# GpSimd and ScalarE stop normalizing k: its norm goes into the gates' exponent, in a gated DeltaNet layer

## The chip, the cores and the metric

The kernel runs on one core of one Trainium2 chip. The metric is the device time of one execution in microseconds (us). Engines are named PE (TensorE, matmuls), DVE (VectorE), ACT (ScalarE), POOL (GpSimd) and SP (SyncE, which issues the DMAs).

## The reference, cut to what matters

One inference step of a two-layer decoder for 512 prompt tokens and 8 single decode tokens (520 columns in all). Layer 0 is a pooling and differential attention mixer, layer 1 a gated DeltaNet mixer with 8 heads; each is followed by a SwiGLU feed-forward. The change lies in layer 1:

```
q = l2_normalize(conv[..q]) * (GDN_DK ** -0.5)
k = l2_normalize(conv[..k])                      # x * rsqrt(sum(x*x) + EPS)
g = -exp(a_log) * softplus(a + dt_bias);  beta = sigmoid(b)
Gc = cumsum(g)                                   # within a chunk
decay = exp(where(i >= j, Gc_i - Gc_j, -inf));  gam = exp(Gc)
M = I + where(i > j, beta_i * (k_i . k_j) * decay, 0)
W = M^-1 (beta * gam * k);   U = M^-1 (beta * v)
qk = (q_i . k_j) * decay;    k_dec = exp(Gc_last - Gc) * k
per chunk:  u = U - W S;  o = (gam q) S + qk u;  S = g_last * S + k_dec^T u
```

## The kernel before, in words

**Layout.** Features lie on the 128 partitions, tokens in the columns. Weights come as f32 units of 1 MB through two `stage` slots, are split into two f16 parts by ACT (`wh`) and DVE (`wl`), and each product is three f16 matmuls by k tile (`wh·zh`, `wh·zl`, `wl·zh`), each in two halves of 260 columns. All engines run hand-written programs in a fixed order; semaphores alone join them, so an instruction that waits holds up everything behind it on its own engine.

**The head loop.** Layer 1's mixer is a loop over the 8 heads, `for h in range(HG)`, on every engine. PE does in head h the DeltaNet work of head h and, between its dependent steps, the projection of head h + 1, cut in 32 parts of 6 matmuls (`fill(n)` does the next n parts; `project_part`, line L2110). In order, PE's head is: `gb_ps`, where a selector matrix spreads the head's rows of cumulated log gates (bank 2) and of beta (bank 3) to all partitions (L2230, f32 at L2222 in head 0), with the same for the 8 decode tokens (L2233); `stat_head` (L2094), the sums for the output norm of head h - 1; `kk_ps` and `qk_ps` (both L2119), k times k and k times q by 128-token chunks; two transposes `n_ps` and `tk_ps` (both L2125); six doubling steps of the triangular inverse, `level(l)`, each a product `z_ps` (L2288), a transpose `x_ps` (L2296) and a product `v_ps` (L2303); at last four chunk steps with `ws_ps` (L2331), `u_ps` (L2315), `ds_ps` (L2345) and the output products (L2347, L2351). In level 0 the decode tokens' products stand as well (L2264 to L2268).

**The norm of k.** After the convolution and SiLU of head p = h + 1, POOL squares k (`square_k`), PE sums the squares over the partitions with a matrix of ones (`stat_l2(p)`, L2087, in the third chunk step of head h), ACT takes Ln and Exp of it (`norm_l2`, L996 and L998) and POOL multiplies k by the result (`normalize_k`, L643). DVE then makes beta·k in `kbg_w` (L1581), which is the left side of `kk_ps`. DVE's exponent of the decay is `et` (four instructions, L1575); ACT takes its Exp (L1053), DVE makes `nt_z`, the off-diagonal matrix (L1586), from which `level` starts. ACT evacuates its transpose to `nf_u` (L1045), POOL makes six copies of pieces of that (`offs`, L709), one for each level, and then multiplies `kbg_w` by `gamB`, the exponent of the gates (L712), gates the output of head h - 1 (L661) and q (L716).

**Other work named below.** `leave` (L1438) scales a finished projection tile; `convolve` (L1453, L1456) is a tap of the convolution; `head_scale` (L1522) belongs to the output norm; `split_quarter` (L1486) is a quarter of DVE's weight split; `next_split` (L761) is ACT's whole weight split of a unit. L1602 evacuates `z_ps`, L1628 takes `v_ps` off the inverse, L1672 is the step of the state S, L1120 ACT's evacuation of the head's output.

## Time and profile before

| | |
|---|---|
| median of 3 runs | 1335.24 us (1335.07 to 1337.36) |
| the profiled execution's own time | 1334.86 us |
| its span in the trace | 1332.9 us |
| granted PE clock, mean | 0.998 |
| busy: PE, PE's weight loads, DVE, ACT, POOL | 98%, 81%, 48%, 38%, 27% |
| DMA traffic over the span | 140.89 MB, mean 106 GB/s |

Busy shares are over the span; the kernel's own time is about 2 us longer, for what lies around it. A matmul's end is modelled with its pipeline, so the records of neighbouring matmuls overlap; what a matmul costs PE is the distance from its start to the next one's start.

### The profile page before, as it was taken

Reading aid. Unit: us, or ns where it says so; the run is one execution under the profiler, and the core shown is the slowest. Engines: PE = TensorE matmul, PEld = TensorE weight load, DVE = VectorE, ACT = ScalarE, POOL = GpSimd, SP = SyncE. Lnnn points to the kernel's source line nnn. Section 1 sums busy time; section 2 is a strip of 40 time slices with the busy share of each in tenths; the row PEclk is TensorE's granted clock in tenths of the full one; section 3 lists DMA queues with packets and bytes.
Section 4 is the critical chain, followed back from the end, with each engine's and each line's share of the span. In section 5 each row is a group of like instructions: output and inputs, shape, how many; then the busy total and the mean of one; then the engine's idle time right before and its main releaser. Section 6 shows DMA issues by size and latency. Waiting matters only on the chain.

```text
span 1332.9 us, 28024 instructions
## 1 busy us (share of the span) xinstructions
PE 1309.3 (98%) x11596; PEld 1086.3 (81%) x11596; DVE 634.4 (48%) x1009; ACT 507.1 (38%) x785; POOL 365.9 (27%) x506
## 2 busy tenths in 40 slices
PE   8999999999999999999999999999999999999997
PEld 7766588888888888887778777877888888888886
DVE  5447653333333322267776677766633333332222
ACT  6243453222222322244555465545432223222221
POOL 1004324121212100165453545453221222211010
PEclk9999999999999999999999999999999999999999
DMA  8658422422232232111212221122223222233211
GB/s 264 209 191 278 143 96 95 149 102 99 94 122 104 101 121 85 63 64 40 89 41 88 88 72 57 73 96 66 96 105 116 94 94 94 94 118 131 88 44 64
DMA packets 32140, 140.89 MB, mean 106 GB/s; under 512 B 4634, under 2 KB 6938, under 8 KB 20155
## 3 DMA queue, kind: packets, MB, share of 16 engines
q1 hardware_dynamic: 32058, 139.75, 30.2%
q8 instruction: 58, 0.95, 0.3%
q14 instruction: 24, 0.19, 0.0%
HBM read 128.63 MB, written 11.11 MB: 105 GB/s over the span
## 4 chain that ended last, share of the span: by engine, by line
PE 92%; DVE 4%; ACT 1%; issue 1%; DMA 1%; SPq 0%; DVEq 0%; ACTq 0%
PE P L1745 64%; PE P L2110 10%; PE P L2303 2%; DVE wl L1486 1%; PE P L2288 1%; PE P L2365 1%; PE P L2296 1%; PE P L2119 1%; PE P L1823 1%; PE P L2125 1%; PE P L2331 1%; PE P L2345 1%; PE P L1955 1%; PE P L2321 1%; PE P L1898 1%
## 5 line engine op out<-in xcount | busy, mean ns | idle before, releaser
L1745 PE MATMUL P<-zh,wh 128*128 128x260 f16 x1712 | 329.2, 273 | 2.1 <-DVE wl L1194 2.1
L1745 PE MATMUL P<-zl,wh 128*128 128x260 f16 x1712 | 329.0, 273 | 0.0
L1745 PE MATMUL P<-zh,wl 128*128 128x260 f16 x1712 | 329.0, 273 | 0.0
L1174 DVE SCALAR_TENSOR_TENSOR wl<-stage,wh 128x2048 f16<-128x2048 f32 (+1 forms) x75 | 185.3, 2471 | 195.4 <-ACT wh L761 192.8
L1745 PE MATMUL P<-arena,wh 128*128 128x260 f16 x1816 | 276.2, 273 | 1.0 <-DVE hT L1391 0.3
L1745 PEld LDWEIGHTS P<-arena,wh 128*128 128x128 f16 x1816 | 175.0, 97 | 29.2 <-issue 1.3
L1745 PEld LDWEIGHTS P<-zh,wh 128*128 128x128 f16 x1712 | 164.3, 97 | 34.0 <-issue 6.7
L1745 PEld LDWEIGHTS P<-zh,wl 128*128 128x128 f16 x1712 | 165.6, 97 | 25.9
L1745 PEld LDWEIGHTS P<-zl,wh 128*128 128x128 f16 x1712 | 165.4, 97 | 25.8
L1745 PE MATMUL P<-arena,wl 128*128 128x260 f16 x908 | 174.5, 273 | 0.0
L761 ACT ACTIVATE wh<-stage 128x2048 f16<-128x2048 f32 (+1 forms) x80 | 161.8, 2023 | 3.6 <-PE P L1745 3.6
L564 POOL TENSOR_TENSOR arena<-arena 128x520 f32<-128x520 f32 x44 | 56.5, 1284 | 359.7 <-DVE arena L1411 359.7
L1411 DVE TENSOR_TENSOR arena<-P,rstd 128x520 f32<-128x520 f32 x88 | 61.2, 696 | 171.8 <-PE P L1745 168.8
L965 ACT ACTIVATE arena<-arena 128x520 f32 (+1 forms) x44 | 28.0, 637 | 198.9 <-POOL arena L564 198.9
L1745 PEld LDWEIGHTS P<-arena,wl 128*128 128x128 f16 x908 | 87.9, 97 | 13.6
L523 POOL TENSOR_TENSOR ssq<-ssq,sq 128x520 f32<-128x520 f32 x27 | 36.8, 1364 | 212.1 <-ACT sq L770 211.9
L2110 PE MATMUL P<-zh,wh 128*128 128x260 f16 x448 | 86.9, 275 | 0.0
L2110 PE MATMUL P<-zl,wh 128*128 128x260 f16 x448 | 86.1, 273 | 0.0
L2110 PE MATMUL P<-zh,wl 128*128 128x260 f16 x448 | 86.1, 273 | 0.0
L961 ACT ACTIVATE arena<-arena 128x520 f32<-128x520 f32 x44 | 28.0, 637 | 129.6 <-DVE arena L1411 129.6
L777 ACT ACTIVATE zh<-hT,par 128x520 f16<-128x520 f32 x24 | 17.4, 726 | 120.9 <-DVE hT L1391 109.2
L1486 DVE SCALAR_TENSOR_TENSOR wl<-stage,wh 128x512 f16<-128x512 f32 x64 | 59.8, 944 | 0.0
(366 smaller groups left out, 1646.3 us busy)
## 6 DMA issues: line engine op xcount, KB each, us to landing
stage<-w_gu SPq DMA_DIRECT2D x44, 1024.0 KB, 4.8
stage<-w_in SPq DMA_DIRECT2D x23, 1024.0 KB, 4.9
stage<-w_dn SPq DMA_DIRECT2D x16, 1408.0 KB, 5.8
arena<-cache_k SPq DMA_DIRECT2D x32, 256.0 KB, 3.5
stage<-w_out SPq DMA_DIRECT2D x8, 1024.0 KB, 5.4
arena<-cache_v SPq DMA_DIRECT2D x32, 256.0 KB, 3.0
arena<-delta_state SPq DMA_DIRECT2D x8, 512.0 KB, 3.5
o_ds<-arena SPq DMA_DIRECT2D x8, 512.0 KB, 6.8
```

The costliest lines, as they stand in the source:

```text
L523: ins = nc.gpsimd.tensor_tensor(ssq[:, :], ssq[:, :], sq[:, k % 2, :], ADD)
L564: nc.gpsimd.tensor_tensor(gu[:, j, :], gt[:, j, :], ut[:, j, :], MUL).then_inc(prod_done, 1)
L761: nc.scalar.activation(wh[:, j, 0:words], stage[:, j, 0:words], ACT.Copy, scale=WS).then_inc(hi_ready, 1)
L777: nc.scalar.activation(zh[:, k, :], hT[:, k, :], ACT.Copy, scale=par[:, NORM[b] + k:NORM[b] + k + 1]).then_inc(z_hi, 1)
L961: nc.scalar.activation(gt[:, j, :], gt[:, j, :], ACT.Silu).then_inc(silu_done, 1)
L965: nc.scalar.activation(fh[:, bass.ds(2 * i + j, 1), :], gu[:, j:j + 1, :], ACT.Copy).then_inc(f_hi, 1)
L1174: nc.vector.scalar_tensor_tensor(out=wl[:, j, 0:words], in0=stage[:, j, 0:words], scalar=WS, in1=wh[:, j, 0:words], op0=MUL, op1=SUB).then ...
L1411: nc.vector.tensor_tensor(paired(dst[:, j, :]), pm[j], paired(rstd[:, :]), MUL).then_inc(pm_free, 1)
L1486: ins = nc.vector.scalar_tensor_tensor(out=wl[:, j, q], in0=stage[:, j, q], scalar=WS, in1=wh[:, j, q], op0=MUL, op1=SUB)
L1745: mm = nc.tensor.matmul(pm[j][:, c, :], w[:, wslot, o:o + 128], x[:, k, c * CH:(c + 1) * CH], start=(k == first and w is wh and x is xh), ...
L2110: mm = nc.tensor.matmul(pm[0][:, c, :], w[:, u % 2, o:o + 128], x[:, k, c * CH:(c + 1) * CH], start=(k == 0 and w is wh and x is zh), stop ...
L2303: mm = nc.tensor.matmul(v_out[:, c % 2, 64 * m:64 * m + 64], dt2_x[r, 128 * m:128 * m + 128], nt_z[r, 64 * m:64 * m + 64], start=True, sto ...
```

## The change

k is left as it is after the SiLU. With n_i = |k_i|², log n_i and log beta_i go into the exponent of the decay, and what is solved for is scaled by |k_i| (`kn`, in place of beta, on v). The diagonal of k·k is the sum of squares, so the norm is read from `kk_ps` (four reductions with an identity matrix on DVE). Beta's row is no longer spread over the prompt's columns; its logarithm comes with the transposed rows (`tokm`). Decode tokens get their norms from one product with the matrix of ones (`qkk`), now 16 columns and part of `gb_ps`. The sum of squares on POOL, `stat_l2`, `norm_l2`, `normalize_k` and DVE's beta·k go. GpSimd now makes `kbg_w` from k and `gamB` (`gate_k`), behind its six copies, as it did the gating of `kbg_w` before. Several orders move: `kk_ps` ahead of `gb_ps`, `add_query` from the end of a head into the next one, ACT's weight split ahead of the Exp of `et`, ACT's load of the SiLU tables behind `Kd`, and the number of projection parts at six places.

```
@@ GpSimd @@
-            def square_k(h):
...
-            def normalize_k(h):
-                pool.wait_ge(nrs, h + 1)
-                x = qkvc[:, h % 2, 1, :]
-                nc.gpsimd.tensor_tensor(x, x, rs2[:, 1, :], MUL).then_inc(nq, 1)
+            def decode_products(h):
+                pool.wait_ge(csilu, 3 * h + 2)
+                if h >= 1:
+                    pool.wait_ge(kqs_ps, h)
+                    pool.wait_ge(*G("gb_ps", h))
+                q, k = qkvc[:, h % 2, 0, SEQ:], qkvc[:, h % 2, 1, SEQ:]
+                nc.gpsimd.tensor_copy(kd2, two(k))
...
+                nc.gpsimd.tensor_tensor(qkk[:, 0:8], q, k, MUL)
+                nc.gpsimd.tensor_tensor(qkk[:, 8:16], k, k, MUL).then_inc(dprep, 1)
+            def gate_k(h):
+                pool.wait_ge(*G("gam", h + 1))
+                if h >= 1:
+                    pool.wait_ge(*G("ws_ps", 3 * h))
+                nc.gpsimd.tensor_tensor(kbg_w, qkvc[:, h % 2, 1, 0:SEQ], gamB, MUL).then_inc(k_gated, 1)
@@ GpSimd, loop @@
                 for l in range(LEVELS):
                     nc.gpsimd.tensor_copy(packed(l, offs[l]), early(l, nf_u)).then_inc(S["om"], 1)
-                pool.wait_ge(*G("gam", h + 1))
-                pool.wait_ge(*G("kk_ps", h + 1))
-                nc.gpsimd.tensor_tensor(kbg_w, kbg_w, gamB, MUL).then_inc(S["kbg"], 1)
+                gate_k(h)
@@ ACT, loop @@
                 act.wait_ge(*G("gb_ps", h + 1))
-                nc.scalar.activation(gamB, P[:, 2, :], ACT.Exp).then_inc(S["gam"], 1)
                 nc.scalar.activation(gD[:, h, :], P[:, 7, 0:8], ACT.Exp).then_inc(S["gd"], 1)
+                nc.scalar.activation(rk, P[:, 7, 24:32], ACT.Ln, bias=epsc[:, 2:3]).then_inc(S["lr"], 1)
+                act.wait_ge(*G("dg", h + 1))
+                nc.scalar.activation(klog, ksq, ACT.Ln, bias=epsc[:, 2:3]).then_inc(S["lk"], 1)
+                act.wait_ge(*G("lr", h + 1))
+                nc.scalar.activation(rk, rk, ACT.Exp, scale=-0.5)
+                nc.scalar.activation(qks, P[:, 7, 16:24], ACT.Copy).then_inc(S["rk"], 1)
+                if h >= 1:
+                    next_split("in1", h, 1)
                 act.wait_ge(*G("ex", h + 1))
                 nc.scalar.activation(et, et, ACT.Exp).then_inc(S["et"], 1)
                 nc.scalar.activation(kd4, d4, ACT.Exp).then_inc(S["kd4"], 1)
+                act.wait_ge(*G("lk", h + 1))
+                nc.scalar.activation(kn, klog, ACT.Exp, scale=0.5).then_inc(S["kn"], 1)
...
-                next_split("in1", h, 1)
+                nc.scalar.activation(gamB, P[:, 2, :], ACT.Exp).then_inc(S["gam"], 1)
@@ DVE, loop @@
-                dve.wait_ge(*G("gd", h + 1))
+                dve.wait_ge(*G("kk_ps", h + 1))
+                for c in range(4):
+                    ins = nc.vector.tensor_tensor_reduce(out=dg_out[c], in0=P[:, 6, c * 128:(c + 1) * 128], in1=ident[:, :],
+                                                         scale=1.0, scalar=0.0, op0=MUL, op1=ADD,
+                                                         accum_out=ksq[:, c:c + 1])
+                ins.then_inc(S["dg"], 1)
+                dve.wait_ge(*G("lk", h + 1))
+                link(nc.vector.tensor_tensor(tj, tokg[:, :, h], klog, ADD))
...
-                nc.vector.tensor_copy(bD[:, h, :], P[:, 7, 8:16]).then_inc(S["bd"], 1)
-                dve.wait_ge(nq, h + 1)
-                nc.vector.tensor_tensor(kbg_w, P[:, 3, :], k, MUL).then_inc(S["kb"], 1)
+                dve.wait_ge(*G("rk", h + 1))
+                nc.vector.tensor_tensor(br, P[:, 7, 8:16], rk, MUL).then_inc(S["bd"], 1)
+                if n >= 0:
+                    add_query(n)
                 convolve(h, 2, 0)
-                convolve(h, 2, 1)
@@ PE, loop @@
+                pe.wait_ge(csilu, 3 * h + 2)
+                if h >= 1:
+                    pe.wait_ge(*G("u", 4 * h))
+                chunks(6, k, k, "kk_ps")
...
-                    for m, t in enumerate((g3, b3)):
-                        nc.tensor.matmul(P[:, 2 + m, :], sel3[0:72, h % 2, :], t[0:72, 0:SEQ], start=True, stop=True)
+                    nc.tensor.matmul(P[:, 2, :], sel3[0:72, h % 2, :], g3[0:72, 0:SEQ], start=True, stop=True)
...
+                pe.wait_ge(dprep, h + 1)
+                nc.tensor.matmul(P[:, 7, 16:32], ones[:, :], qkk, start=True, stop=True).then_inc(S["gb_ps"], 1)
                 fill(4 if h < HG - 1 else 3)
+                ready(h, "gd", "rk", "bd")
+                chunks(7, k, q, "qk_ps")
+                ready(h, "kn")
                 if h >= 1:
-                    pe.wait_ge(nln, h + 1)
+                    pe.wait_ge(snew, h)
                     stat_head(h - 1)
-                pe.wait_ge(nq, h + 1)
-                ready(h, "kb")
...
-                        if c == 2:
+                        if c == 2 and h == HG - 1:
                             pe.wait_ge(snew, h + 1)
-                            if h + 1 < HG:
-                                stat_l2(h + 1)
...
                     if c == 0:
-                        fill(3)
+                        fill(2 if h < HG - 1 else 3)
```

PE's order at the turn from one head to the next (heads 1 and 2), before. The row before the first is the last output product; `head_act`, `head_dve` and the like are the semaphores on which the other engines count their head tiles:

```order
L2351 MATMUL P<-arena 128x128
L2230 MATMUL P<-arena 128x512 [waits head_dve,head_pool]
L2230 MATMUL P<-arena 128x512
L2233 MATMUL P<-arena 128x8 [waits head_act]
L2233 MATMUL P<-arena 128x8
...
L2094 MATMUL P<-ssq,onesH 128x260 [waits o1sum,nln]
L2094 MATMUL P<-ssq,onesH 128x260
L2119 MATMUL P<-arena 128x128 [waits head_dve,nq]
L2119 MATMUL P<-arena 128x128 x3
L2119 MATMUL P<-arena 128x128 [waits head_dve,head_act]
L2119 MATMUL P<-arena 128x128 x3
```

And of the changed kernel at the same place (L2124 is `chunks`, L2236 the gates' selector, L2242 the product with ones, L2099 `stat_head`):

```order
L2350 MATMUL P<-arena 128x128
L2124 MATMUL P<-arena 128x128 [waits head_act,csilu]
L2124 MATMUL P<-arena 128x128 x3
L2236 MATMUL P<-arena 128x512 [waits head_dve,head_pool]
L2239 MATMUL P<-arena 128x8 [waits head_act]
L2239 MATMUL P<-arena 128x8
L2242 MATMUL P<-arena,ones 128x16 [waits dprep]
...
L2124 MATMUL P<-arena 128x128 [waits head_dve,head_act]
L2124 MATMUL P<-arena 128x128 x3
L2099 MATMUL P<-ssq,onesH 128x260 [waits o1sum,snew,head_act]
L2099 MATMUL P<-ssq,onesH 128x260
```

The k·k products moved to the head's first place, one selector matmul of 512 columns went, and the sums of `stat_head` now also wait for ACT (`kn`).

ACT's order in the front of head 2, before (L1050 is `gamB`, L1051 `gD`, L1053 `et`, L1055 the copy of the identity, L761 the weight split, L1027 and L1029 `head_factor`):

```order
L1050 ACTIVATE arena<-P 128x512 [waits head_pe]
L1051 ACTIVATE arena<-P 128x8
L1053 ACTIVATE arena<-arena 128x512 [waits head_dve]
L1054 ACTIVATE arena<-arena 128x4
L1055 ACTIVATE arena<-ident 128x512
L761 ACTIVATE wh<-stage 128x2048 [waits mm_done,w_in1]
L1027 ACTIVATE arena<-P,epsc 128x520 [waits o1stat]
```

And of the changed kernel (L1046 to L1051 are the logarithms and factors of the norms, L763 the weight split, L1055 `et`, L1058 `kn`, L1062 `gamB`):

```order
L1045 ACTIVATE arena<-P 128x8 [waits head_pe]
L1046 ACTIVATE arena<-P,epsc 128x8
L1048 ACTIVATE P<-arena,epsc 128x4 [waits head_dve]
L1050 ACTIVATE arena<-arena 128x8 [waits head_act]
L1051 ACTIVATE arena<-P 128x8
L763 ACTIVATE wh<-stage 128x2048 [waits mm_done,w_in1]
L1055 ACTIVATE arena<-arena 128x512 [waits head_dve]
L1056 ACTIVATE arena<-arena 128x4
L1058 ACTIVATE arena<-P 128x4 [waits head_act]
L1059 ACTIVATE arena<-ident 128x512
L1062 ACTIVATE arena<-P 128x512
L1021 ACTIVATE arena<-P,epsc 128x520 [waits o1stat]
```

The weight split moved from behind the Exp of `et` to ahead of it, and `gamB` from first to nearly last.

## Rows read from the trace of the kernel before

**Rows 1.** The page: busy time by engine, and the chain that ended last.

```profile
PE 1309.3 (98%) x11596; PEld 1086.3 (81%) x11596; DVE 634.4 (48%) x1009; ACT 507.1 (38%) x785; POOL 365.9 (27%) x506
...
PE 92%; DVE 4%; ACT 1%; issue 1%; DMA 1%; SPq 0%; DVEq 0%; ACTq 0%
```

**Rows 2.** Windows, one head: length, PE, PEld, DVE, ACT, POOL; clock, DMA share, GB/s.

```profile
681.00:725.00 44.00, 43.26 (x405) 34.73 (x404) 31.88 (x69) 23.55 (x50) 20.48 (x37) 1.00 0.21 73
```

**Rows 3.** Timeline of PE, front of head 2 (start, duration, line, shapes, records).

```profile
678.96 0.39 PE L2351 MATMUL P<-arena 128*128 128x128 f32 x2
679.43 0.59 PE L2230 MATMUL P<-arena 72*128 72x512 bf16 x2
680.04 0.20 PE L2233 MATMUL P<-arena 72*128 72x8 bf16 x2
680.14 0.38 PE L2110 MATMUL P<-zh,wh 128*128 128x260 f16 x2
...
682.82 1.04 PE L2094 MATMUL P<-ssq,onesH 128*128 128x260 f32 x4
683.69 1.95 PE L2119 MATMUL P<-arena 128*128 128x128 f32 x16
...
689.13 0.46 PE L2288 MATMUL P<-arena 128*64 128x64 f32 x8
```

**Rows 4.** Timeline of PE, third chunk step of head 2: `stat_l2` and what follows.

```profile
717.92 1.04 PE L2087 MATMUL P<-sq,ones 128*128 128x260 f32 x4
718.79 0.38 PE L2315 MATMUL P<-arena 128*128 128x128 f32 x2
```

**Rows 5.** Timeline of PE, where head 0 begins.

```profile
589.46 1.04 PE L2087 MATMUL P<-sq,ones 128*128 128x260 f32 x4
...
590.71 1.96 PE L2222 MATMUL P<-arena 40*128 40x512 f32 x4
592.51 0.51 PE L2224 MATMUL P<-arena 40*128 40x8 f32 x4
```

**Rows 6.** Timeline of DVE, front of head 2 and its levels 0 and 1.

```profile
678.94 0.35 DVE L1672 SCALAR_TENSOR_TENSOR arena<-arena,P 128x128 f32<-128x128 f32 x1 [1.50 <-PE P L2345]
...
681.30 1.12 DVE L1575 SCALAR_TENSOR_TENSOR arena<-P,arena 128x128 f32<-128x128 f32 x4
...
689.63 0.29 DVE L1602 TENSOR_TENSOR arena<-P,arena 128x128 f32<-128x128 f32 x1
...
692.44 0.49 DVE L1628 TENSOR_TENSOR arena<-arena,P 128x128 f32<-128x128 f32 x2 [0.92 <-PE P L2303]
692.84 1.60 DVE L1486 SCALAR_TENSOR_TENSOR wl<-stage,wh 128x512 f16<-128x512 f32 x1
```

**Rows 7.** Timeline of ACT, front of head 2.

```profile
679.38 0.60 ACT L1120 ACTIVATE arena<-P 128x512 f32<-128x512 f32 x1 [1.06 <-PE P L2351]
...
681.03 0.17 ACT L1051 ACTIVATE arena<-P 128x8 f32<-128x8 f32 x1
...
683.67 1.89 ACT L761 ACTIVATE wh<-stage 128x2048 f16<-128x2048 f32 x1
```

**Rows 8.** Timeline of DVE in layer 0: the kernel's other multiply-and-reduce.

```profile
43.81 0.29 DVE L1243 CUSTOM_DVE_ANT_0 arena<-P,arena 128x128 f32<-128x128 f32 x1 [1.60 <-PE P L1823]
44.03 0.08 DVE L1243 DVE_READ_ACCUMULATOR2_ANT arena<- 128x1 f32 x1
```

**Rows 9.** Timeline of POOL in head 2: the six copies, the gating of `kbg_w`.

```profile
688.12 2.86 POOL L709 COPY arena<-arena 128x256 f32<-128x256 f32 x6 [4.94 <-ACT arena L1045]
690.94 1.70 POOL L712 TENSOR_TENSOR arena<-arena 128x512 f32<-128x512 f32 x1
```

**Rows 10.** Timeline of DVE ahead of head 0: the gates' rows.

```profile
581.27 0.69 DVE L1471 TENSOR_TENSOR arena<-arena 8x520 f32<-8x520 f32 x1
...
586.60 0.13 DVE L1478 COPY arena<-arena 8x8 f32<-8x8 f32 x1
```

**Rows 11.** Timeline of ACT ahead of head 0: the SiLU of q and k.

```profile
586.77 1.16 ACT L1005 ACTIVATE arena<-arena 128x520 f32<-128x520 f32 x2
```

More of the change, by code:

```diff
@@ L63 @@
 HEAD_TILES = {
-    "pe": ["gb_ps", "kk_ps", "qk_ps", "n_ps", "tk_ps"] + ["z_ps", "x_ps", "v_ps"] * 4 + ["z_ps", "tv_ps", "x_ps", "v_ps"] +
+    "pe": ["kk_ps", "gb_ps", "qk_ps", "n_ps", "tk_ps"] + ["z_ps", "x_ps", "v_ps"] * 4 + ["z_ps", "tv_ps", "x_ps", "v_ps"] +
           ["z_ps", "x_ps", "v_ps"] + ["u_ps", "ds_ps"] + ["ws_ps", "u_ps", "ds_ps"] * 3 + ["o_ps"],
-    "act": ["gam", "gd", "et", "kd4", "yi", "ye", "nf", "kd", "x"] + ["ye", "x"] * 4 + ["bv", "ye", "x"] + ["u"] * 4 + ["o"],
-    "dve": ["ex", "bd", "kb", "nt", "xt", "at"] + ["z", "xt"] * LEVELS + ["s"] + ["r", "s"] * 3,
-    "pool": ["selb"] + ["om"] * LEVELS + ["kbg", "qd"],
+    "act": ["gd", "lr", "lk", "rk", "et", "kd4", "kn", "yi", "gam",
+            "ye", "nf", "kd", "x"] + ["ye", "x"] * 4 + ["bv", "ye", "x"] + ["u"] * 4 + ["o"],
+    "dve": ["dg", "ex", "bd", "nt", "xt", "at"] + ["z", "xt"] * LEVELS + ["s"] + ["r", "s"] * 3,
+    "pool": ["selb"] + ["om"] * LEVELS + ["qd"],
 }
@@ L201, in hybrid_trunk @@
         qq = [sq[:, 0, :], rs2[:, 0, :]]
-        gD, bD = (a2(64).rearrange("p (h b) -> p h b", h=HG) for _ in range(2))
+        tokg = rs2[:, 1, 0:32].rearrange("p (c n) -> p c n", c=4)
+        ksq, kn, tj = (rs2[:, 1, 32 + 4 * i:36 + 4 * i] for i in range(3))
+        klog = P[:, 4, 400:404]
+        rk, br, qks = (rs2[:, 1, 48 + 8 * i:56 + 8 * i] for i in range(3))
+        gD = a2(64).rearrange("p (h b) -> p h b", h=HG)
         gate = a2(8)
@@ L222, in hybrid_trunk @@
         tailw = ddt.bitcast(f16).rearrange("p (m k n c) -> p m k n c", m=2, k=KD - EARLY_K, n=2)
+        dg_out = [t[:, i:i + 128] for t in (dt2_x, ya) for i in (256, 384)]
         bf40 = [t.bitcast(mybir.dt.bfloat16) for t in (yn1[:, 0:260], yn1[:, 260:520], ors1[:, 0:260])]
@@ L706, in _ @@
                                         ).then_inc(sdec, 1)
+                if h == 0:
+                    tail_of(0, 2)
+                    decode_conv(0, (2,))
                 pool.wait_ge(*G("nf", h + 1))
@@ L1063, in _ @@
                 evac(nf_u, 3, "n_ps", "nf", h)
-                act.preload_act_table(ACT.Silu)
                 act.wait_ge(*G("tk_ps", h + 1))
@@ L1070, in _ @@
                 ins.then_inc(S["kd"], 1)
+                act.preload_act_table(ACT.Silu)
                 for l in range(LEVELS):
@@ L1113, in _ @@
                         act.preload_act_table_set("natural_log_exp_and_others")
-                    if c == 2 and p < HG:
-                        norm_l2(p)
                 if p < HG:
@@ L2083, in _ @@
             unit("in1", 0, 1, zh, zl)
-            def stat_l2(h):
-                pe.wait_ge(nsq, h + 1)
-                for c in range(2):
-                    mm = nc.tensor.matmul(stat[:, c, :], ones[:, :], sq[:, 1, c * CH:(c + 1) * CH],
-                                          start=True, stop=True)
-                mm.then_inc(nstat, 1)
             def stat_head(h):
@@ L2143, in stat_last @@
                 mm.then_inc(o1stat, 1)
-            stat_l2(0)
             pe.wait_ge(rows_ready, 2)
             for c in range(4):
-                mm = nc.tensor.transpose(P[:, 6, 40 * c:40 * c + 40], rows[0:40, c * 128:(c + 1) * 128],
+                mm = nc.tensor.transpose(P[:, 5, 40 * c:40 * c + 40], rows[0:40, c * 128:(c + 1) * 128],
                                          ident[0:40, 0:40])
@@ L2220, in _ @@
                 if h == 0:
-                    for m in range(2):
-                        nc.tensor.matmul(P[:, 2 + m, :], selb[0:40, m, :], rows[0:40, 0:SEQ], start=True, stop=True)
+                    nc.tensor.matmul(P[:, 2, :], selb[0:40, 0, :], rows[0:40, 0:SEQ], start=True, stop=True)
                     for m in range(2):
@@ L2266, in between @@
                                              start=True, stop=True)
-                        nc.tensor.matmul(P[:, 4, 256:264], ones[:, :], qkp, start=True, stop=True)
                         nc.tensor.transpose(P[0:36, 4, 264:392], kpad[:, 0:36], ident[:, :]).then_inc(kqs_ps, 1)
```

104 lines of the change are left out of this document (42 added, 62 removed).

## The prediction

> **What bounds the kernel now.** I read the page first: PE is busy for 98% of the span and makes up 92% of the chain that ended last, while no other engine passes 48% [rows 1]. So what the change takes off DVE, ACT or POOL is worth nothing by itself; it counts where it takes matmuls off PE, or where PE stands still. Next the windows, one per head: in 44.0 us PE is busy 43.26, so at most 0.74 us a head is plainly idle, at full clock [rows 2]. Then the timelines of the engines around the turn from head 1 to head 2, for the waits inside those 0.74 us.
>
> There the reader should take starts, not durations, since ends are modelled. Eight 128-column f32 matmuls take 0.22 us each at PE (683.69, and the parts behind them); `stat_l2` with its two of 260 columns takes 717.92 to 718.79, 0.87 us [rows 3, 4]. The last output product starts at 678.96, so PE could go on at 679.18. It goes on at 679.43, just after DVE's state step L1672 ends at 679.29: 0.25 us idle. The two selector matmuls (512 columns each, 0.22 us by the same pace of columns) are through by 679.87, and the small ones start at 680.04, behind ACT's evacuation, which ends at 679.98: 0.17 us idle [rows 3, 6, 7]. Four projection parts then take 680.14 to 682.82, 0.67 us each, and level 0 starts at 689.13 [rows 3].
>
> **What the change removes from PE.** `stat_l2` goes eight times (once ahead of head 0, then in heads 0 to 6): 8 x 0.87 = 7.0 us [rows 4, 5]. It stood between two chunk steps, where a projection part of 0.67 us now fills the wait, moved there from the first chunk step; the parts are 32 in either kernel, so they cost nothing more. Beta's selector matmul goes eight times: in head 0 it is f32, half of 590.71 to 592.51, 0.90 us; in the others 0.22 us [rows 5]. The product with ones gets 16 columns for 8 and moves from level 0 to the front; I leave its cost unchanged, some 0.2 us like a short matmul pair, at either place.
>
> **What it does to the front of a head**, in head 2's times, as if it began at the same 679.18. Now `kk_ps` comes first: 0.89 us, to 680.07. It covers both waits, the one on L1672 and the one on ACT's evacuation. Selector 0.22, small ones 0.1, ones 0.2: 680.6, against 680.14 before. Four parts: 683.27. Meanwhile the new chain runs:
> - DVE, four reductions. The trace has the same kind of instruction over a 128x128 block: 0.22 us from one to the next, then 0.08 for the accumulator [rows 8]. 4 x 0.22 + 0.08 = 0.95, so 680.17 to 681.1.
> - ACT, the logarithm of four numbers: 0.17, like the 8-column L1051 [rows 7]; 681.3. DVE, the sum `tj`, 0.2 with its link; then the four `et` instructions, 1.12 [rows 6]; `ex` and `bd` end with two short ones at 0.15, a little over L1478's 0.13 [rows 10]: 682.9. PE asks for `bd` at 683.27, so it is hidden, with 0.35 us to spare.
> - ACT, in the same time: three short ones (681.1 to 681.6), the weight split 1.89 [rows 7] to 683.5, Exp of `et` 0.60 (512 columns, like L1120), `kd4` and `kn` at 0.17: 684.45. PE is through with `qk_ps` at 684.16 and asks for `kn` ahead of `stat_head`: a new wait of 0.3 us. Behind that wait stand `stat_head`, one part and the transpose `n_ps`; POOL's copies wait for the latter's evacuation.
> - PE goes on: `stat_head` 0.87, one part 0.67, two transposes of four blocks each (0.11 us a block, a single pass) 0.88, three parts 2.0: level 0 at 688.9, against 689.13. 0.23 us are gained, and 0.2 more in level 0, where the ones product no longer stands.
>
> DVE has then to keep up in levels 0 and 1. It has one tap more between `At` and the tile that it must free, but it waited 0.92 us for PE in level 0 [rows 6], and it loses beta·k. `decode_update` gets one short instruction more (0.2 us), inside a wait of DVE for PE. POOL: `gate_k` is one instruction of the size of the one it replaces, at the same place, 1.70 us behind 2.86 us of copies [rows 9], and nobody asks for it before the second chunk step, far later. POOL's squares and its normalization end, and were waited for by nobody late. All of this costs nothing, by the cover named.
>
> **Sum.** Heads 1 to 6: 0.43 + 0.87 = 1.30 us each, 7.8. Head 7 has no `stat_l2`: 0.43. Head 0: 0.87 ahead of it, 0.90 for the selector, 0.87 in it, 2.64; against that two new waits. The rows of beta need three more DVE instructions (0.48, 0.48 and 0.69, the size of L1471) ahead of ACT's Exp, and another of 0.69 behind, so what ended at 586.60 ends some 2.5 us later, about when PE is through at 589.46; the SiLU of q and k, at 586.77, moves by some 2 us, and `kk_ps` waits for it to 589.95: 0.5 us [rows 5, 10, 11]. In head 0 the split of weights still stands ahead of the logarithms, so `bd` is about 0.35 us late. Head 0: 1.8 us. Together 10.0 us. The profiled execution took 1334.86 us, which gives 1324.8; the median of the runs is 0.4 above it, so I say 1325.
>
> **Bounds.** The chain's unknown is how fast three engines hand short work to each other. Below: nothing is late, `kn` included (0.3 us less a head, 2 us in all), and head 0's waits vanish: 1322. Above: every step of the new chain takes twice as long (the reductions 1.9 for 0.95), given below as a rival. I take the rows' values, since the reduction is seen in this very kernel.
>
> **Rivals.**
> - *The new chain is late* (18%). With reductions of 1.9 us `bd` comes at 683.9 (0.6 us of wait), the split ends at 684.45 and `kn` comes at 685.4, 0.65 us after PE's `qk_ps`: 1.25 us idle for 0.3, so 0.95 us a head over seven heads, 6.7 us back: 1331.5. For it: the chain crosses PE, DVE, ACT, DVE, ACT, PE within 5 us. Against: the parts cover 2.7 of these.
> - *The front's gain is lost in levels 0 and 1* (14%). There DVE's weight split takes 1.60 us, and PE waits for DVE rather than the other way round. If POOL, whose copies start when ACT has evacuated `n_ps`, and DVE stay where they are, 0.43 us a head go, 3.4 us: 1328.5. The Trainium skill, "SBUF — State Buffer", on who interferes with whom, says that a DVE instruction with two SBUF inputs and a GpSimd instruction that reads SBUF exclude each other for the whole of an instruction. As a mechanism of this kernel: the third tap moves under the six copies, 0.48 us each (2.86 / 6), and DVE could come one or two copies late to the evacuation of `z_ps` [rows 9]. By that rule it is 0.5 to 1 us late. PE needs that evacuation only after a transpose and a part, so about 1.2 us are free, and by this the sum stays as it is.
> - *Slower* (7%). In the trace the weight split starts at 683.67, behind the Exp of `et` [rows 7]; nothing shows that its weights were there earlier. In the changed kernel `et` stands behind it. Were the split possible only then, it would end at 685.56, `kn` would come at 686.5, and PE would stand 2.35 us for 0.3: 7 x 2.05 = 14.4 us, more than the whole gain: 1339. It decides from 683.67 - 681.6 - (10.0 / 7) on, that is, if the weights are there later than 683.0. Against: that half of `stage` was freed in the head before, and DMA is nearly idle here, 0.21 of its time [rows 2].
> - *No difference* (5%): the first two together, and head 0 worse than reckoned: 1333 to 1336.
> - Forecast as summed (56%): 1322 to 1327.
>
> **Range and chances.** The forecast's range is 1322 to 1327. With the two rivals above it, 8 in 10 lie from 1321.5 to 1331.5. Within 0.2% (2.7 us), about what a measurement of this kernel can tell from no change, of the time before, lie the no-difference case and the edge of the first rival: 0.07. Slower: 0.07. Faster: the rest of the first rival, the second and the forecast, 0.86.
>
> **What would show it.** In the profile after: a head from start to start of `et`'s group takes about 42.6 us, not 43.9; PE's first f32 group after the output products has no idle ahead of it; eight groups of `stat_l2` are gone and nothing stands in their place; the gap ahead of `stat_head` is about 0.3 us and is put down to ACT; the gap ahead of `qk_ps` is nothing in heads 1 to 7 and some 0.35 us in head 0. The prediction fails if PE stands for over 1 us in the front of each head, or if the waits of levels 0 and 1 on DVE grow by what the front gained.

## The result, and the profile after

The changed kernel takes 1320.14 us (median of 4 runs, 1318.96 to 1322.66) against 1335.15 us (median of 4) for the kernel before in the same measurement: a ratio of 0.9885, 95% interval 0.9872 to 0.9899. It is faster by 15.0 us where 10.2 were forecast, and lies below the forecast's range and below the one of 8 in 10. The profiled execution took 1319.1 us, its span is 1317.4 us, 15.5 less than before; the forecast's sum was 10.0.

The page of the changed kernel, with the lines that answer to [rows 1]:

```profile
PE 1297.6 (98%) x11555; PEld 1078.9 (82%) x11555; DVE 641.4 (49%) x1086; ACT 501.3 (38%) x809; POOL 351.7 (27%) x498
...
PE 94%; DVE 3%; issue 1%; DMA 1%; ACT 1%; SPq 0%; DVEq 0%
```

PE's busy time fell by 11.7 us and the span by 15.5: more waiting went than the forecast's list contains.

Next, a head is cut in three pieces, all read from starts in PE's timeline: **front**, from the end of the last output product (its start and 0.22 us) to the first `z_ps` (level 0); **levels 0 and 1**, up to the `z_ps` of level 2; and the rest. PE, changed kernel, where [rows 3] stood (last output product, `kk_ps`, selector, small ones, ones product, first part, `qk_ps`, `stat_head`, and the `z_ps` of levels 0, 1 and 2):

```profile
673.76 0.39 PE L2350 MATMUL P<-arena 128*128 128x128 f32 x2
673.98 1.06 PE L2124 MATMUL P<-arena 128*128 128x128 f32 x8
674.87 0.38 PE L2236 MATMUL P<-arena 72*128 72x512 bf16 x1
675.09 0.19 PE L2239 MATMUL P<-arena 72*128 72x8 bf16 x2
675.14 0.37 PE L2242 MATMUL P<-arena,ones 128*128 128x16 f32 x2
675.37 0.38 PE L2115 MATMUL P<-zh,wh 128*128 128x260 f16 x2
...
678.05 1.05 PE L2124 MATMUL P<-arena 128*128 128x128 f32 x8
679.03 1.14 PE L2099 MATMUL P<-ssq,onesH 128*128 128x260 f32 x4
...
683.66 0.46 PE L2289 MATMUL P<-arena 128*64 128x64 f32 x8
...
687.09 0.45 PE L2289 MATMUL P<-arena 128*64 128x64 f32 x8
...
689.97 0.45 PE L2289 MATMUL P<-arena 128*64 128x64 f32 x8
```

The front is 673.98 to 683.66, 9.68 us, and PE goes from the output product into `kk_ps` with no gap. And PE of the kernel before in levels 0 and 1 of the same head (rows that were not shown ahead of the prediction): the `z_ps` of level 1, then two instructions that wait for DVE. Ahead of them, in level 0, the transpose `x_ps`.

```profile
690.65 0.41 PE L2296 MATMUL P<-ident,arena 128*128 128x128 f32 x2
...
693.03 0.45 PE L2288 MATMUL P<-arena 128*64 128x64 f32 x8
...
694.79 0.66 PE L2303 MATMUL P<-arena 64*128 64x64 f32 x8 [0.25 <-DVE arena L1602]
...
696.57 0.45 PE L2288 MATMUL P<-arena 128*64 128x64 f32 x8 [0.34 <-DVE arena L1628]
```

`x_ps` starts 0.32 us behind the last of the decode tokens' products (690.33). It waits for ACT's `Kd` (L1068, to 690.51), which stands behind the load of the SiLU tables:

```profile
688.07 1.28 ACT L1064 ACT_TABLE_LOAD   x1
689.37 1.14 ACT L1068 ACTIVATE arena<-P,arena 128x128 f32<-128x128 f32 x4
```

In the changed kernel `Kd` ends at 683.41, before z0, and the same distance is 0.12 us (684.62 to 684.74).

By head, in us (z0, z1, z2: start of the `z_ps` of levels 0, 1, 2). A head is counted from its z0 to the next head's, so the front in its row is the one that leads to the next head:

| | front | z0 to z1 | z1 to z2 | rest | head |
|---|---|---|---|---|---|
| before, every head from 1 to 5 | 9.95 | 3.90 | 3.53 | 26.50 | 43.88 |
| changed, heads 1, 2, 3, 5 ("quick") | 9.68 | 3.43 | 2.87 | 25.62 | 41.60 |
| changed, head 4 ("long") | 9.68 | 4.05 | 3.38 | 25.62 | 42.73 |
| forecast | 9.72 | 3.70 | 3.53 | 25.63 | 42.58 |

Front and rest came as forecast. Levels 0 and 1, where only the 0.2 us of the moved ones product had been expected, gave 1.13 us in a quick head and nothing in a long one. Head 6 is long too (4.06 and 3.37). Outside the table, the front of head 1 took 10.28 us before and takes 9.68 now. The windows from z0 to z2, a quick head (2) and a long one (4) of the changed kernel; columns as in [rows 2]:

```profile
683.66:689.97 6.31, 6.31 (x79) 4.63 (x78) 5.83 (x12) 3.73 (x9) 6.31 (x8) 1.00 0.01 4
766.87:774.30 7.43, 6.50 (x79) 4.66 (x78) 7.33 (x12) 3.73 (x9) 6.43 (x8) 1.00 0.01 2
```

The clock is full in both, DMA is silent, the same instructions run. What differs is DVE: 7.33 us busy for 5.83 with the same 12 instructions, and PE stands for 0.93 us.

DVE in these two stretches, first the quick head, behind the dots the long one (L1528 `head_scale`, L1492 a quarter of the weight split, L1642 the subtraction off the inverse):

```profile
684.58 0.75 DVE L1528 SCALAR_TENSOR_TENSOR arena<-arena,par 128x520 f32<-128x520 f32 x1
685.25 0.88 DVE L1492 SCALAR_TENSOR_TENSOR wl<-stage,wh 128x512 f16<-128x512 f32 x1
686.50 0.49 DVE L1642 TENSOR_TENSOR arena<-arena,P 128x128 f32<-128x128 f32 x2 [0.37 <-PE P L2304]
686.91 0.92 DVE L1492 SCALAR_TENSOR_TENSOR wl<-stage,wh 128x512 f16<-128x512 f32 x1
...
767.79 1.01 DVE L1528 SCALAR_TENSOR_TENSOR arena<-arena,par 128x520 f32<-128x520 f32 x1
768.72 1.75 DVE L1492 SCALAR_TENSOR_TENSOR wl<-stage,wh 128x512 f16<-128x512 f32 x1
770.40 0.47 DVE L1642 TENSOR_TENSOR arena<-arena,P 128x128 f32<-128x128 f32 x2
770.79 1.38 DVE L1492 SCALAR_TENSOR_TENSOR wl<-stage,wh 128x512 f16<-128x512 f32 x1
```

And POOL (L714 the six copies, L683 `gate_k`, L667 the gating of the output), first the quick head, then the long one:

```profile
682.45 3.15 POOL L714 COPY arena<-arena 128x256 f32<-128x256 f32 x6 [4.74 <-ACT arena L1038]
685.56 1.71 POOL L683 TENSOR_TENSOR arena<-arena 128x512 f32<-128x512 f32 x1
687.22 1.74 POOL L667 TENSOR_TENSOR arena<-arena 128x520 f32<-128x520 f32 x1
...
765.66 2.59 POOL L714 COPY arena<-arena 128x256 f32<-128x256 f32 x6 [4.74 <-ACT arena L1038]
768.21 1.71 POOL L683 TENSOR_TENSOR arena<-arena 128x512 f32<-128x512 f32 x1
```

PE in the long head, the `z_ps` of levels 1 and 2:

```profile
770.92 0.45 PE L2289 MATMUL P<-arena 128*64 128x64 f32 x8 [0.55 <-DVE arena L1642]
...
774.30 0.45 PE L2289 MATMUL P<-arena 128*64 128x64 f32 x8 [0.34 <-DVE arena L1642]
```

Read them side by side. The first split quarter takes 0.88 us in the quick head and 1.75 in the long one. In the quick head the six copies take 3.15 us, so the sixth ends 1.9 us after z0 and DVE's quarter, begun 1.6 us after z0, has gone ahead of `gate_k`. In the long head the copies take 2.59, `gate_k` begins 1.34 us after z0, the quarter is begun 0.51 us behind it, and ends 0.55 us after `gate_k` is over. So I read them thus: the two engines take turns instruction by instruction; who begins first has it, and the other's record grows by what it waited.

### The profile page after: what moved, and what is told of

The parts are those of the page before. It is cut to its first block, busy times and chain, and to the rows that moved or that the text cites. A ratio compares the mean times of both kernels' runs of the same rounds, so it can differ in the third digit from the quotient of the medians.

```text
span 1317.4 us, 27997 instructions
## 1 busy us (share of the span) xinstructions
PE 1297.6 (98%) x11555; PEld 1078.9 (82%) x11555; DVE 641.4 (49%) x1086; ACT 501.3 (38%) x809; POOL 351.7 (27%) x498
## 4 chain that ended last, share of the span: by engine, by line
PE 94%; DVE 3%; issue 1%; DMA 1%; ACT 1%; SPq 0%; DVEq 0%
PE P L1757 65%; PE P L2115 11%; PE P L2304 2%; PE P L2289 1%; PE P L2124 1%; PE P L2364 1%; PE P L2130 1%; PE P L2297 1%; DMA hT<-xT 1%; PE P L2333 1%; PE P L1835 1%; PE P L2344 1%; PE P L2322 1%; PE P L1967 1%; DVE wl L1492 1%
## 5 line engine op out<-in xcount | busy, mean ns | idle before, releaser
L763 ACT ACTIVATE wh<-stage 128x2048 f16<-128x2048 f32 (+1 forms) x80 | 161.8, 2023 | 3.6 <-PE P L1757 3.6
L1492 DVE SCALAR_TENSOR_TENSOR wl<-stage,wh 128x512 f16<-128x512 f32 x64 | 60.1, 949 | 0.0
```

Of the source, the lines that this page charges most:

```text
L763: nc.scalar.activation(wh[:, j, 0:words], stage[:, j, 0:words], ACT.Copy, scale=WS).then_inc(hi_ready, 1)
L1492: ins = nc.vector.scalar_tensor_tensor(out=wl[:, j, q], in0=stage[:, j, q], scalar=WS, in1=wh[:, j, q], op0=MUL, op1=SUB)
```

## The experiments

Theory A, formed from these rows: in levels 0 and 1 PE doesn't set the pace. Three long instructions of POOL and four quarters of DVE shut each other out, and what PE has there is partly slack. Most of the 1.13 us of a quick head came since DVE now comes in time. Theory B: PE sets the pace there too, and the surplus comes from PE's own work. Ratios are to the kernel before on the same chip. "Head" is the length of the heads between 1 and 5 unless said otherwise.

**A product as long as `stat_l2`, back in the third chunk step** (four f32 matmuls of 128 columns with a matrix of ones, result unused, in heads 0 to 6):

```
+                        if c == 2 and h < HG - 1:
+                            for i in range(4):
+                                nc.tensor.matmul(P[:, 4, 0:128], ones[:, :], onesH[:, :], start=True, stop=True)
```

> The changed kernel with four f32 matmuls of 128 columns more (a matrix of ones, 0.88 us by the trace's 0.22 each) in the third chunk step of heads 0 to 6, where stat_l2 stood. Both theories expect the same here: nothing else moves, each head is 0.88 us longer, 6.2 us in all, 1326.3 against the changed kernel's 1320.1. It prices the removed sums.

Measured: 1325.53 us, ratio 0.9922 [0.9906, 0.9937]. Heads are 42.50 (quick) and 43.62 (long): 0.9 more of each kind. There PE's work costs its full length, as the sum had it.

**The same four matmuls in level 0** of the changed kernel:

```
                     if l == 0:
                         pe.wait_ge(sdec, h + 1)
+                        if h < HG - 1:
+                            for i in range(4):
+                                nc.tensor.matmul(P[:, 6, 0:128], ones[:, :], onesH[:, :], start=True, stop=True)
```

> The same four matmuls, but in level 0 of heads 0 to 6. Theory (the extra gain is a matter of phase between DVE's weight split and GpSimd's gating: when PE and DVE come to level 1 earlier, the split at L1492 starts ahead of GpSimd's gating of the output and takes 0.9 us instead of 1.6): DVE's second split quarter starts after GpSimd's second long instruction and takes 1.6 us again, so the matmuls cost more than their own 0.88, about 1.4 to 1.5 us a head, 10 to 10.8 us in all, 1330 to 1331. Rival (PE alone sets the head): 0.88 us a head as in the third chunk step, 1326.3.

Measured: 1324.69 us, 0.9922 [0.9905, 0.9939]. Levels 0 and 1 are 4.52 + 2.91 = 7.43 us in every steady head: 1.13 more than a quick head, and nothing more than a long one. At this place the four matmuls take 1.09 us from start to start (685.57 to 686.66 in head 2), so a quick head pays for them in full, and no more. What I expected of DVE did not happen: its second quarter takes 0.97 us, not 1.6, and it is the first that takes 1.76, as in a long head. The total is 5 to 6 us under what I expected, and under the rival's too: a head paid 1.13 us and not 1.4 to 1.5, and I had not counted that the changed kernel has long heads already.

**And in level 0 of the kernel before**, the same edit:

> The kernel before with the four f32 matmuls of ones (0.88 us on PE) added in level 0 of heads 0 to 6. Theory (in the kernel before, level 0 to level 2 takes 7.43 us because GpSimd's three long instructions and DVE's three weight split quarters take turns, and PE has slack there): the matmuls cost at most 0.1 to 0.2 us a head, level 0 to 2 stays within 7.4 to 7.6 us, 1335.2 to 1336.5 in all. Rival (PE sets the time there too, as it is busy for 98%): 0.88 us a head, 6.2 us, 1341.4.

Measured: 1336.6 us, 1.0006 [0.9997, 1.0015]; heads of 44.00 us. The four matmuls, 1.09 us from start to start here too (692.65 to 693.74), cost 0.12 us a head. Theory B asked for 0.88 a head, 6 us in all, and falls: 0.97 us of the 1.09 went into waiting that was already there. Levels 0 and 1 are 4.75 + 2.81 us. DVE in head 2 of this kernel, and behind it POOL:

```profile
696.43 0.49 DVE L1628 TENSOR_TENSOR arena<-arena,P 128x128 f32<-128x128 f32 x2 [1.77 <-PE P L2306]
696.83 0.75 DVE L1486 SCALAR_TENSOR_TENSOR wl<-stage,wh 128x512 f16<-128x512 f32 x1
```

```profile
695.74 1.29 POOL L661 TENSOR_TENSOR arena<-arena 128x520 f32<-128x520 f32 x1
696.99 1.72 POOL L716 TENSOR_TENSOR arena<-arena 128x512 f32<-128x512 f32 x1
```

DVE now waits 1.77 us for PE, where it waited 0.92 [rows 6], and its quarter takes 0.75 us where it took 1.60: it asks at 696.83, just ahead of POOL's handover at 696.99, and hardly waits.

**`gate_k` ahead of the six copies, changed kernel:**

```
+                gate_k(h)
                 pool.wait_ge(*G("nf", h + 1))
                 for l in range(LEVELS):
                     nc.gpsimd.tensor_copy(packed(l, offs[l]), early(l, nf_u)).then_inc(S["om"], 1)
-                gate_k(h)
```

> The changed kernel with gate_k ahead of the six copies instead of behind. Theory (phase): GpSimd's two remaining long instructions then run 1.7 us earlier, the gating of q holds from about 12.9 to 14.6 us after the head's start, just as DVE's second split quarter (12.93) wants to begin; that one ends at about 15.2 instead of 13.85 and PE comes 0.5 to 0.7 us later to level 2: 3.5 to 5 us slower in all, 1324 to 1325. Rival (any instruction of GpSimd taken off that stretch only helps DVE, or does nothing): 1317 to 1320.

Measured: 1322.18 us, 0.9893 [0.9877, 0.9909]. All steady heads are alike, 41.95 us (3.43 + 3.22). So the order on POOL alone changes the length of level 1, by 0.35 us against a quick head where I had said 0.5 to 0.7, and the total is 2 us under what I expected.

**The same in the kernel before** (the gating of `kbg_w` ahead of the copies):

```
+                pool.wait_ge(*G("gam", h + 1))
+                pool.wait_ge(*G("kk_ps", h + 1))
+                nc.gpsimd.tensor_tensor(kbg_w, kbg_w, gamB, MUL).then_inc(S["kbg"], 1)
                 pool.wait_ge(*G("nf", h + 1))
                 for l in range(LEVELS):
                     nc.gpsimd.tensor_copy(packed(l, offs[l]), early(l, nf_u)).then_inc(S["om"], 1)
-                pool.wait_ge(*G("gam", h + 1))
-                pool.wait_ge(*G("kk_ps", h + 1))
-                nc.gpsimd.tensor_tensor(kbg_w, kbg_w, gamB, MUL).then_inc(S["kbg"], 1)
```

> The kernel before with its gating of kbg_w ahead of the six copies. Theory (phase): in it the third split quarter takes 1.55 us behind GpSimd's gating of q; with that gating 1.7 us earlier it takes 0.7, while the second stays near 1.6. PE comes 0.5 to 0.8 us earlier to level 2 in heads 1 to 7: 1330 to 1332 against 1335.2. Rival (the head is set by PE, GpSimd's place has no part in it): 1335.

Measured: 1332.64 us, 0.9975 [0.9966, 0.9984], heads of 43.16 us (3.90 + 2.81). One instruction moved on an engine that is busy for 27% of the span takes 0.72 us off a head, all of it in level 1. Level 0 keeps its 3.90. The median lies a little above the 1330 to 1332 that I expected.

**POOL's long instructions out of levels 0 and 1**, changed kernel, `gate_k` and the gating of q held until level 2:

```
-                gate_k(h)
                 if n >= 0:
                     gate_out(n)
+                pool.wait_ge(*G("z", LEVELS * h + 3))
+                gate_k(h)
```

> The changed kernel, but on GpSimd the output's gating comes right behind the six copies, and gate_k and the gating of q wait until DVE has passed the evacuation of level 2's first product (a wait on DVE's counter), so that they don't meet DVE's three weight split quarters of levels 0 and 1. Theory (whichever of GpSimd's long two-input instructions and DVE's split comes first holds up the other; a head of the changed kernel takes 41.61 us when the copies end late and 42.73 us when gate_k starts ahead of the first quarter): the quarters take 0.7 to 0.9 us, level 0 to level 2 takes at most the 6.3 us of the quick heads in every head, no head takes 42.7; 1317 to 1319 and less spread. Rival (the long heads come from something else, such as the order of ACT): two kinds of heads stay, 1320 to 1321.

Measured: 1345.82 us, 1.0078 [1.0065, 1.0091], slower than the kernel before. Levels 0 and 1 did as theory A says, 3.43 + 2.81 = 6.24 us in heads 0 to 6 and quarters of 0.68 to 0.99 us. But level 2 went from 3.01 to 5.16 us. DVE there, in head 2 (the update for the decode tokens):

```profile
693.86 0.17 DVE L1541 TENSOR_TENSOR arena<-P,arena 128x8 f32<-128x8 f32 x1
694.06 1.10 DVE L1542 TENSOR_TENSOR arena<-arena 128x8 f32<-128x8 f32 x1
695.19 1.19 DVE L1543 TENSOR_TENSOR arena<-arena 128x8 f32<-128x8 f32 x1
696.42 1.09 DVE L1544 TENSOR_TENSOR arena<-arena 128x8 f32<-128x8 f32 x1
```

and POOL beside it (L683 `gate_k`, L720 the gating of q, L671 the low f16 part of the gated output):

```profile
693.87 1.27 POOL L683 TENSOR_TENSOR arena<-arena 128x512 f32<-128x512 f32 x1 [3.44 <-DVE arena L1617]
695.09 1.27 POOL L720 TENSOR_TENSOR arena<-arena 128x512 f32<-128x512 f32 x1
696.32 1.17 POOL L671 TENSOR_TENSOR arena<-arena 128x520 f16<-128x520 f32 x1
```

Three instructions of 8 columns, 0.17 us each in the changed kernel, take 1.09 to 1.19 us: each ends just after the POOL instruction beside it. In two of the heads the cost was larger still, which the last section tells.

**`gate_k` ahead, only the gating of q held until level 2:**

```
+                gate_k(h)
                 pool.wait_ge(*G("nf", h + 1))
...
-                gate_k(h)
...
+                pool.wait_ge(*G("z", LEVELS * h + 3))
                 pool.wait_ge(*G("qk_ps", h + 1))
```

> The changed kernel with gate_k ahead of the six copies and only the gating of q held until DVE has passed level 2's evacuation. Theory: as above, one long instruction (the output's gating, 1.28 us) is left near the quarters; level 0 to level 2 at most 6.3 us, 1317 to 1319. Rival (gate_k ahead costs what it cost in gate_ahead_after, whatever follows): 1322.

Measured: 1330.5 us, 0.9952 [0.9938, 0.9965]. Levels 0 and 1 again 6.24, level 2 at 4.14 to 4.31: the same collision, one POOL instruction smaller (in head 2 two of DVE's 8-column instructions take 1.10 and 1.09 us). Both expectations were wrong in the total for the same reason: I had moved POOL's work without asking what DVE does where it lands.

**The load of the SiLU tables back ahead of `Kd`, changed kernel:**

```
                 evac(nf_u, 3, "n_ps", "nf", h)
+                act.preload_act_table(ACT.Silu)
...
                 ins.then_inc(S["kd"], 1)
-                act.preload_act_table(ACT.Silu)
```

> The changed kernel with ACT's load of the SiLU tables put back ahead of Kd. Theory (the 0.2 us between the decode products and the transpose x_ps of level 0 was PE's wait for Kd, and went because the load of 1.28 us moved): the gap is back at 0.2 us a head, or more since PE now comes earlier, 1.6 us or some more in all by itself: 1321.5 to 1323. Rival (the gap was something else): 1320.

Measured: 1321.99 us, 0.9889 [0.9875, 0.9904]; two steady heads of 41.82 (3.71 + 2.81), the other three long. Level 0 is 0.28 us longer and level 1 gives 0.06 back, so in a head that is not long the edit costs 0.22 us. PE's distance ahead of `x_ps` is 0.37 us there (645.47 to 645.84, head 1) for 0.12. The total fits what I expected, but says little, since more heads are long here than in the first profile of the changed kernel.

**The table load behind `Kd`, and the SiLU of z behind `x`'s evacuation, kernel before:**

```
-                act.preload_act_table(ACT.Silu)
...
                 ins.then_inc(S["kd"], 1)
+                act.preload_act_table(ACT.Silu)
...
-                    else:
-                        silu_z(h)
...
                     if l == 0:
+                        silu_z(h)
                         silu_v(h)
```

> The kernel before with only the one order changed: ACT's load of the SiLU tables behind Kd, and the SiLU of z behind the evacuation of x_ps. Theory (PE's 0.2 us ahead of x_ps in level 0 is a wait for Kd): it goes, 0.2 us a head from level 0 to level 1, 1.6 us in all, 1333.6 against 1335.2, unless DVE's quarters take it back. Rival (that gap is not Kd's): 1335.2.

Measured: 1335.79 us, 1.0004 [0.9995, 1.0013]. Level 0 became 4.36 and level 1 3.07, which is again 7.43. PE's gap ahead of `x_ps` fell from 0.32 to 0.19 us, but the table load (690.49 to 691.77) now holds up ACT's evacuation of `x_ps` (L1076, at 691.78), and PE waits for that:

```profile
692.22 0.66 PE L2302 MATMUL P<-arena 64*128 64x64 f32 x8 [0.52 <-ACT arena L1076]
```

So the edit traded one wait for ACT against a longer one and is no clean test of the 0.2 us. Level 0 grew by 0.46 us by it, level 1 shrank by 0.46, and the sum of both didn't move by 0.01: the end of level 1 is not set by when PE gets there.

**`kk_ps` behind `gb_ps` as before the change, changed kernel:**

```
-    "pe": ["kk_ps", "gb_ps", "qk_ps", ...
+    "pe": ["gb_ps", "kk_ps", "qk_ps", ...
```

with the four `kk_ps` lines moved behind the ones product.

> The changed kernel with kk_ps behind gb_ps, ahead of the four projection parts, as no cover for the two waits at the turn of the heads. By the prediction's own steps: the waits on the state step (0.25) and on ACT's evacuation (0.17) are back, and the chain over the reductions, the logarithm and the weight split starts about 0.8 us later, so that PE waits about 0.4 us for kn: 0.8 us a head, 5 to 6 us in all, 1325 to 1326. Rival (these waits are covered otherwise): 1320.

Measured: 1327.74 us, 0.9935 [0.992, 0.9949]; every steady head 42.82, the levels those of a quick head (3.43 + 2.87). The front grew by 1.21 us, not 0.8, read from start to start in head 2: PE stands 0.25 us for the state step, 0.39 for ACT's evacuation, 0.39 for `bd`, and 0.10 more than in the changed kernel at `kn`, and `kk_ps` itself takes 0.09 more. `kk_ps` as a cover is worth more than the 0.42 us of gaps that I read in [rows 3], since the norm's chain starts at it.

**`gate_k` ahead, the gating of q held only until level 1's `z` is evacuated:**

```
+                gate_k(h)
                 pool.wait_ge(*G("nf", h + 1))
...
-                gate_k(h)
...
+                pool.wait_ge(*G("z", LEVELS * h + 2))
                 pool.wait_ge(*G("qk_ps", h + 1))
```

> The changed kernel with gate_k ahead of the six copies and the gating of q held until DVE has passed the evacuation of level 1's first product (one level earlier than in gate_k_ahead_q_late, where it fell on the decode tokens' short instructions). Theory: the third split quarter then starts ahead of the gating of q and takes 0.7 to 0.9 us, the gating ends ahead of decode_update; level 0 to level 1 is 3.43, level 1 to 2 2.8 to 2.9, level 2 to 3 3.0 in every head, no head is longer than 41.65: 1317.5 to 1319.5. Rival (the moved gating meets another instruction of DVE that PE waits for): 1322 or more.

Measured: 1318.85 us, 0.9876 [0.9861, 0.9891]. All steady heads are 41.55 (3.43 + 2.82, level 2 3.01). POOL in head 2 (L715 the six copies):

```profile
682.52 1.57 POOL L683 TENSOR_TENSOR arena<-arena 128x512 f32<-128x512 f32 x1 [2.35 <-ACT arena L1063]
684.91 3.95 POOL L715 COPY arena<-arena 128x256 f32<-128x256 f32 x6 [0.82 <-ACT arena L1039]
688.82 1.29 POOL L667 TENSOR_TENSOR arena<-arena 128x520 f32<-128x520 f32 x1
690.94 1.65 POOL L720 TENSOR_TENSOR arena<-arena 128x512 f32<-128x512 f32 x1 [0.83 <-DVE arena L1617]
```

`gate_k` now lies ahead of level 0, under PE's transposes and parts, the copies wait in small pieces (3.95 us for 2.59 to 3.15), and the third quarter takes 0.68 us, as expected. The second still takes 1.29 beside the output's gating, where PE doesn't have to wait for it.

**The changed kernel once more, unedited:**

> The changed kernel as it is, again, beside the others on one chip. If its heads come in two kinds (41.61 and 42.73 us), its time is 1318 to 1323 by how many of the long kind there are, and the profiled time is 1317.7 + 1.12 x (number of long heads) to within 0.5. If instead the spread is noise of the whole chip, the times of the kernel before spread alike and the count of long heads doesn't follow the time.

Measured beside the last one: 1320.7 us (1317.81 to 1323.46), 0.988 [0.9865, 0.9895]. The profiled run took 1323.46 us and has five long heads (1 to 5), where the first profile has two (4 and 6). Three more long heads are 3.4 us, and head 0's level 0 starts 0.9 us later (601.27 for 600.37): together 4.3, and the two profiles differ by 4.4. The formula of the expectation gives 1323.3 for this profile, and 1319.9 for the first, which took 1319.1. So between these two profiles most of the difference is how many heads turned out long. It isn't all of a kernel's spread: the kernel before, in whose profile heads 1 to 5 are all alike, went from 1334.71 to 1337.84 us in the same measurement, against 5.65 us here. The version with q behind level 1 has no long head and the lower median, but the two intervals overlap: that its heads are shorter is shown, that it is faster in all is not.

## Why the prediction was wrong

**What held.** The front: by the sum `qk_ps` stood 4.09 us behind the last output product and level 0 at 9.72; measured are 4.07 and 9.68. `kk_ps` covers both waits, the selector is one, the gaps are gone. The norm's chain is the one costed, as DVE's and ACT's rows of head 2 show (answering to [rows 6, 7, 8]):

```profile
675.08 0.29 DVE L1582 CUSTOM_DVE_ANT_0 arena<-P,ident 128x128 f32<-128x128 f32 x1 [0.38 <-PE P L2124]
...
677.65 0.16 DVE L1594 TENSOR_TENSOR arena<-P,arena 128x8 f32<-128x8 f32 x1
```

```profile
676.04 0.27 ACT L1048 ACTIVATE P<-arena,epsc 128x4 f32<-128x4 f32 x1 [0.15 <-DVE arena L1582]
...
676.40 1.90 ACT L763 ACTIVATE wh<-stage 128x2048 f16<-128x2048 f32 x1
...
678.82 0.16 ACT L1058 ACTIVATE arena<-P 128x4 f32<-128x4 f32 x1
```

The reductions come 0.21 us apart (0.22 in layer 0). The weight split starts 2.42 us into the head, just where the sum had it, so its weights were there, and the "slower" rival falls. `kn` is ready at 5.00 us (5.27 in the sum), and between `qk_ps` and `stat_head` PE's starts leave 0.09 us beyond the 0.89 us of `qk_ps`, not 0.3. The rest of a head gained 0.88 us, `stat_l2`'s 0.87; the experiment in the third chunk step confirms that price. A long head gained 1.15 us, about the forecast 1.30 less the moved product, whose absence was worth nothing there.

Up to level 0 of head 0 the gain is 0.95 us (601.32 to 600.37) and the sum gives 0.92, but this is luck. PE ends the projections ahead of head 0 0.38 us later than before (589.84 for 589.46), and from there to level 0 the gain is 1.33. The wait of 0.35 us ahead of `qk_ps` in head 0, which the sum had, isn't there: `qk_ps` starts at 595.78, 0.22 us behind the last matmul of the parts. One price of a rival was off by itself: the front's 0.43 us stands in the sum for seven heads, not eight, so the loss of it would have been 3.0 us and not 3.4.

**The step that failed** is "DVE has then to keep up in levels 0 and 1 ... All of this costs nothing, by the cover named". It treats both levels as stretches where PE sets the time and in which only the ones product could be saved. In the kernel before they were not. The shortest that these levels come out in any run is 3.43 + 2.81 = 6.24 us; with the ones product, 0.24 us by its rows, that makes 6.48 for the kernel before, which took 7.43. So 0.95 us a head was waiting, and the experiment with the four matmuls confirms it: 6.48 + 1.09 = 7.57 us, measured 7.56. Of this, 0.72 us lie in level 1, in the two places where the rows of PE above show a wait for DVE, which POOL held up; With the gating of `kbg_w` ahead of the copies, just these 0.72 were gone. 0.20 lie in level 0 ahead of `x_ps`, a wait for ACT's `Kd` behind the table load.

I had put the one row with 1.60 us in [rows 6] down as the split's own duration. It is 0.68 us when nothing is in its way. I had even named the turn-taking, in the second rival, and asked only what it might cost; that it already cost something, and could be given back, was not asked. And for the table load's new place behind `Kd`, one of the change's moved orders, the sum had no term at all. Of the 1.13 us of a quick head 0.24 are the ones product, which the sum had at 0.2, about 0.20 to 0.22 the table load, and 0.66 (3.53 to 2.87) the end of the waiting for DVE in level 1.

How it came to be given back can be followed in offsets from z0. POOL's turn in head 2, before:

```profile
692.61 1.28 POOL L661 TENSOR_TENSOR arena<-arena 128x520 f32<-128x520 f32 x1
```

Before, `v_ps` of level 0 stands at 2.53 us, DVE's next quarter at 3.71, and POOL had turned to the gating of the output at 3.48: DVE is 0.23 us late and waits it out. In the changed kernel's quick head `v_ps` stands at 2.07 and the quarter at 3.25, while POOL turns at 3.56: DVE is 0.31 us early and goes first. Of the 0.46 us, 0.24 are the ones product gone from level 0 and 0.20 the gap ahead of `x_ps` (0.12 us for 0.32), which comes back (0.37) when the table load is put back ahead of `Kd`. POOL's own instructions are the same.

**In sum**, by the profiled spans: up to level 0 of head 0, 0.95 us (sum: 0.92); from there to level 0 of head 7, 13.77 (8.9: seven times `stat_l2`, seven fronts, level 0 of heads 1 to 6); behind it, 0.78 (0.2, level 0 of head 7). Of the surplus, 4.87 us lie in the middle stretch: 0.97 to 1.13 in each of the quick heads 0, 1, 2, 3 and 5, -0.17 and -0.01 in the long ones (4 and 6). In head 0 only 0.78 of the 1.13 lie in its levels 0 and 1; 0.37 lie in the front that follows, which was longer before than the others and lost 0.60 us. The range's lower end had been drawn for a chain that is never late, not for a gain in another place, and 1322 was therefore too high.

**What stays open.** Why one head is long and the next quick. The copies begin 1.21 us ahead of z0 in both kinds and `head_scale` 0.92 us behind it, the same to 0.01 us; then either it or the sixth copy goes first (it takes 0.75 us or 1.01). What tips it is below what the trace resolves. In the kernel before all steady heads fall the same way, in most of the variants too. Also open is why four matmuls with the matrix of ones take 1.09 us in level 0 and 0.89 in the third chunk step.

## What to carry to other kernels

Where two engines can shut each other out, a record's duration contains the waiting, and no idle time shows it: compare the same form of instruction in different places, and take the shortest as its price before calling a stretch bound by the third engine. A stretch that takes the same total while PE's work in it is shifted (7.43 us in four kernels here) is not PE's, until PE's work passes that total (7.56 with 1.09 us more). Give every order that a change moves a term in the sum, a table load on a third engine too. Before an engine's long work is moved out of the way, look at what runs beside it in its new place, short instructions above all: they pay the whole of the other's length.
